# Query weights loaded in the last pair of the prompt attention, and the first stream's latents loaded in the query phase

## What is computed

```python
def mla_project(h, pos, p):
    cq, ckv, kr = jnp.split(h @ p['w_in'], [384, 384 + 256], axis=-1)
    cq, ckv = rmsnorm(cq, g_qa), rmsnorm(ckv, g_kva)
    q = (cq @ w_q_up).reshape(B, T, 8, 128 + 64)
    qn = rmsnorm(q[..., :128], g_qn)
    qr = rope(rmsnorm(q[..., 128:], g_qr), pos)
    return qn, qr, ckv, rope(rmsnorm(kr, g_kr), pos)

def mla_sample_mixer(h, pos, past_ckv, past_kpe, p):
    qn, qr, ckv_new, kr_new = mla_project(h, pos, p)
    ckv_all = jnp.concatenate([past_ckv, ckv_new], axis=1)
    kn = rmsnorm(einsum('bkl,lhd->bkhd', ckv_all, w_uk), g_kn)
    o = mla_attend(qn, qr, kn, kr_all, ckv_all, pos, k_pos)   # softmax over keys
    return einsum('bqhl,lhd->bqhd', o, w_uv) @ w_o
```

## The time and the profile before

| | |
|---|---|
| profiled execution, its own time | 2899.37 us |
| its span | 2897.5 us |
| TensorE busy | 2742.1 us, 95% of the span |
| VectorE, ScalarE, GpSimd busy | 1842.4, 1143.5, 890.8 us |
| granted TensorE clock, mean | 0.983 |

### The profile page before, as it was taken

How to read it: one execution, slowest core, us unless ns; L and a number is a source line. 1 busy time by engine, 2 the same in 40 slices (tenths; PEclk the granted TensorE clock), 3 DMA queues, 4 the chain that set the end, 5 groups by cost and what they waited for, 6 DMA issues and landing times.

```text
span 2897.5 us, 46606 instructions
## 1 busy us (share of the span) xinstructions
PE 2742.1 (95%) x15902; PEld 2455.4 (85%) x15902; DVE 1842.4 (64%) x3070; ACT 1143.5 (39%) x2373; POOL 890.8 (31%) x970
## 2 busy tenths in 40 slices
PE   7889998779998999999999999999999999999998
PEld 4878777678887799999998988888889998989997
DVE  4577787545555567676767677323576767676685
ACT  3355555424444234343434323323233434344331
POOL 1122011036664003433434254000002435253435
PEclk9999999879999999999999999999999999999999
DMA  5144334322223421111111139114521111111118
GB/s 216 55 174 163 120 130 140 107 71 66 65 82 118 152 88 44 43 43 43 43 43 43 43 78 267 64 44 138 175 95 44 43 43 43 43 57 44 43 58 145
DMA packets 121468, 255.10 MB, mean 88 GB/s; under 512 B 16036, under 2 KB 66116, under 8 KB 118024
## 3 DMA queue, kind: packets, MB, share of 16 engines
q1 hardware_dynamic: 112408, 221.70, 22.9%
q0 software_dynamic: 8944, 31.86, 5.0%
HBM read 213.39 MB, written 40.12 MB: 87 GB/s over the span
## 4 chain that ended last, share of the span: by engine, by line
PE 64%; DVE 1%; DMA 1%; SPq 1%; issue 0%; POOL 0%; ACT 0%; POOLq 0%; DVEq 0%; ACTq 0%
PE psum L109 21%; PE psum L111 21%; PE psum L110 21%; PE psum L3033 1%; PE psum L3174 1%; PE psum L3185 0%; PE psum L3148 0%; DMA scratch_x_mid<-half_x 0%; DMA gate_wu_raw<-in_cm_w_in 0%; SPq L2189 0%; DMA half_m<-scratch_mixT 0%; DVE half_out L2786 0%; DVE half_w_lo L2655 0%; DMA half_x<-in_x 0%; SPq L2184 0%
## 5 line engine op out<-in xcount | busy, mean ns | idle before, releaser
L109 PE MATMUL psum<-half_hT_hi,half_w_hi 128*128 128x384 f32 x1536 | 513.7, 334 | 0.0
L111 PE MATMUL psum<-half_hT_hi,half_w_lo 128*128 128x384 f32 x1536 | 513.4, 334 | 0.0
L110 PE MATMUL psum<-half_hT_lo,half_w_hi 128*128 128x384 f32 x1536 | 513.3, 334 | 0.0
L2537 POOL TENSOR_TENSOR half_acc<-half_acc,half_upd 128x512 f32<-128x512 f32 x312 | 422.8, 1373 | 33.5 <-ACT half_upd L2306 28.9
L111 PE MATMUL psum<-half_w_hi,half_s_lo 128*128 128x512 f32 x1040 | 405.7, 390 | 0.0
L110 PE MATMUL psum<-half_w_lo,half_s_hi 128*128 128x512 f32 x1040 | 405.6, 390 | 0.0
L109 PE MATMUL psum<-half_w_hi,half_s_hi 128*128 128x512 f32 x1040 | 405.3, 390 | 0.0
L2753 DVE TENSOR_TENSOR half_acc<-half_acc,psum 128x512 f32<-128x512 f32 x416 | 279.4, 682 | 80.9 <-PE psum L111 80.8
L2289 ACT ACTIVATE half_s_raw<-psum 128x384 f32<-128x384 f32 (+2 forms) x256 | 97.7, 407 | 563.8 <-PE psum L111 563.8
L109 PEld LDWEIGHTS psum<-half_hT_hi,half_w_hi 128*128 128x128 f32 x1536 | 288.3, 188 | 1.2
L110 PEld LDWEIGHTS psum<-half_hT_lo,half_w_hi 128*128 128x128 f32 x1536 | 288.3, 188 | 1.2
(11 more groups left out here) (406 smaller groups left out, 5776.0 us busy)
## 6 DMA issues: line engine op xcount, KB each, us to landing
half_w_raw<-in_w SPq DMA_DIRECT2D x64, 512.0 KB, 4.2
half_w_raw<-in_w SPq DMA_DIRECT2D x128, 256.0 KB, 3.5
patt_mod_w<-in_ada_w_ffn SPq DMA_DIRECT2D x32, 768.0 KB
patt_mod_w<-in_ada_w_att SPq DMA_DIRECT2D x16, 1024.0 KB, 5.6
half_m<-scratch_mixT SPq DMA_DIRECT2D x18, 512.0 KB, 5.0
satt_lT_raw<-in_cacheT SPq DMA_DIRECT2D x32, 256.0 KB, 3.0
satt_l_raw<-in_cache POOLq DMA_DIRECT2D x32, 256.0 KB, 3.5
half_w_raw<-in_w_o SPq DMA_DIRECT2D x16, 512.0 KB, 5.5
```

The source lines that it names most:

```text
L109: pe.matmul(out, a_hi, b_hi, start=first, stop=False)
L110: pe.matmul(out, a_hi, b_lo, start=False, stop=False)
L111: return pe.matmul(out, a_lo, b_hi, start=False, stop=last)
L2537: pool.tensor_tensor(part, part, a.upd[n % UPDS][:], ALU.add).then_inc(a.added, 1)
```

## The change

- A new object `Ahead` holds four tiles and their 14 semaphores, made before the prompt attention, and does their loads. `Phase.ended` leaves those semaphores out of what is cleared.
- In the prompt attention's last pair, after the store of group 3, SyncE loads the query weights (4 chunks) and the key weights (2 pieces), 3.3 MB.
- In every pair, SyncE's store of adaLN step 3, with the load of the next pair's first table, stands after the store of group 6 instead of after that of group 7.
- The query phase starts with the query chunks instead of the key weights. Its per-head work is cut into two halves of four heads: root, normalisation, rotation, transposes, eviction, and product with `wukT`. The sums of squares stand between the splits. The keys' sum, root and `rn_wide` come after the queries'. SyncE loads the constants first, then `wukT`, then stream 0's latents and rope keys (8 loads), which the sample attention no longer loads.
- In the sample attention, VectorE's `split_m(0)` moves from the last stream's tile 7 to tile 6. Token tile 3's rows are loaded there, after `m_ready` 2 and before the store of the sample rows, and the first phase of `mlp_stages` no longer loads them for layer 0.
- Tiles have other places in SBUF.

```diff
@@ prompt_attention_phase, SyncE
+                        if g == 3 and last:
+                            sp.wait_ge(proj_ready, 1 + PAIRS * T)
+                            sp.wait_ge(ss_ready, 1 + PAIRS * T)
+                            ahead.load_query_weights(sp, io)
                         if g == 5 and not last:
                             load_mod1_w(p, 4)
-                    store_mod1(p, 3, not last)
+                        if g == 6:
+                            store_mod1(p, 3, not last)
@@ class Ahead
+    def load_query_weights(self, sp, io):
+        for c in range(4):
+            cols = slice(c * 2 * (DN + DR), (c + 1) * 2 * (DN + DR))
+            sp.dma_start(self.wq_raw[:, :, cols], io["w_q"][:, :, cols]).then_inc(self.wq_in[c], 16)
+        for i in range(2):
+            sp.dma_start(self.wuk_raw[:, i, :], io["w_uk"][:, i, :]).then_inc(self.wuk_in[i], 16)
@@ sample_query_phase, SyncE
-                for i in range(2):
-                    sp.dma_start(wuk_raw[:, i, :], io["w_uk"][:, i, :]).then_inc(wuk_in[i], 16)
-                for c in range(4):
-                    sp.dma_start(wq_raw[:, :, chunk(c)], io["w_q"][:, :, chunk(c)]).then_inc(wq_in[c], 16)
-                sp.dma_start(wukT[:], io["w_ukT"]).then_inc(wukT_in, 16)
                 (five constants)
+                sp.dma_start(wukT[:], io["w_ukT"]).then_inc(wukT_in, 16)
+                for q in range(4):
+                    ahead.load_latents(sp, io, 0, q)
+                    ahead.load_positions(sp, io, 0, q)
@@ GpSimd
-                pool.wait_ge(kss_ready, 1)
-                rms(slice(2, 3), kr_ready)
-                pool.wait_ge(ss_ready, 4)
-                rms(slice(0, 2), r_ready)
+                for half in range(2):
+                    pool.wait_ge(ss_ready, 2 * half + 2)
+                    rms(slice(0, 2), heads(half), r_ready)
+                pool.wait_ge(kss_ready, 1)
+                rms(slice(2, 3), slice(0, H), kr_ready)
@@ ScalarE (wq_split, squares and the key weights' loop as before, each in a function)
+                for c in range(3):
+                    wq_split(c)
+                squares(0)
+                wq_split(3)
+                squares(1)
+                (wuk split, i = 0, 1)
+                squares(2)
+                squares(3)
                 (squares of the keys)
-                act.wait_ge(qT_raw, 1)
-                act.activation(qnT[:], ...)
-                act.activation(qrT[0:DR, :, :]..., ...).then_inc(qT_ready, 1)
+                for half in range(2):
+                    act.wait_ge(qT_raw, half + 1)
+                    act.activation(qnT[:, heads(half), :], ...)
+                    act.activation(qrT[0:DR, :, :]...[:, :, heads(half), :], ...).then_inc(qT_ready, 1)
@@ VectorE
+                for c in range(3):
+                    wq_split(c)
+                sums(0)
+                wq_split(3)
+                sums(1)
+                (wuk low parts, i = 0, 1)
+                sums(2)
+                sums(3)
                 dve.wait_ge(const_in, 16 * 5)
-                step.then(dve.tensor_tensor(gg[:], g_qn[:], g_kn[:], ALU.mult))
+                step.run(dve.tensor_tensor(gg[:], g_qn[:], g_kn[:], ALU.mult))
+                tokens_of(0)
+                tokens_of(1)
                 dve.wait_ge(ksq_ready, 1)
                 (sum of the keys' squares, then ckv_f and kr_f)
@@ TensorE
+                (queries, chunks 0 to 3, then the keys)
+                for half in range(2):
+                    pe.wait_ge(qtok_ready, half + 1)
+                    (transposes of four heads, qn and qr)
+                    mm.then_inc(qT_raw, 1)
+                pe.wait_ge(ksq_ready, 1)
                 pe.wait_ge(wukT_in, 16)
+                for half in range(2):
+                    pe.wait_ge(qT_ready, half + 1)
+                    (product with wukT, four heads, two k)
@@ sample_attention_phase, SyncE
-                sp.wait_ge(a.m_ready, 1)
-                load_m(2)
+                for t in (2, 3):
+                    sp.wait_ge(a.m_ready, t - 1)
+                    load_m(t)
@@ VectorE
+                        if t == T - 2 and not nxt:
+                            split_m(0)
                         if t == T - 1 and not nxt:
-                            split_m(0)
                             split_wo(0)
@@ mlp_stages, SyncE
-                    if t + 3 < TT:
+                    if t + 3 < TT and not (a.layer == 0 and t == 0):
                         load_m(a, t + 3)
```

213 lines of the change are left out of this document (113 added, 100 removed).

## The result

| | before | after |
|---|---|---|
| median of the runs | 2901.98 us (2898.24 to 2908.42, 4 runs) | 2867.14 us (2866.97 to 2870.05, 4 runs) |
| profiled execution, its span | 2899.37, 2897.5 us | 2866.97, 2865.3 us |
| TensorE busy; granted clock in the query phase | 2742.1; 0.66 | 2733.6; 0.76 |

The ratio is 0.988, 95% interval 0.9861 to 0.9899. With all later runs the medians are 2903.1 (63 runs of before, its repeats included) and 2869.9 (12 runs of after): 33.2 us.

The account below looks back on a forecast made before the run. TensorE, busy for 95% of the span, was taken as the bound, so only its gaps could be won. 7.0 + 14.4 + 0 + 0.9 + 4.2 = 26.5 us off 2903.1 gave 2877 us, range 2868 to 2888.

Parts of the forecast that it names:

- Part 1: Prompt attention pairs: adaLN store behind group 6 removes TensorE's waits for the table; 7.0 us, bounds 0 and 7.8.
- Part 3: Query phase: earlier start, weights already there and work in halves shorten the chain; 14.4 us booked, bounds 9 and 17.
- collision: Query phase: GpSimd's roots beside VectorE's two-input operations delay the chain; 1 us taken off the gain.
- rival (c): Query phase: TensorE stays warm, narrow matmuls at full clock save 5 us, total 2872; chance 0.08.
- Part 2: Last pair: 3.3 MB of weight loads delay group 4's store, but nobody waits; cost 0, cover 4 us.
- part 4: Sample attention's start: loading stream 0's latents ahead gains nothing, transfers were there already; 0, bounds 0 and +1.
- Part 5: Sample attention's end: `split_m(0)` one tile earlier takes VectorE's 1.22 us off the last tile; 0.9 us, bounds 0 and 1.5.
- part 6: MLP stages' start: token tile 3 loaded earlier removes TensorE's 2.54 us wait and cold start; 4.2 us, bounds 2.5 and 4.5.

Follow-up runs that it names:

- part 6 alone: Only token tile 3's rows loaded earlier, in the sample attention, against the kernel before: 2899.12 us, ratio 0.9987.

## Why the prediction was right and where it was wrong

**Part 1: the term that was mis-sized.** The mechanism is the one described: the wait for the table went, nothing took its place, and the phase started earlier (1.05 us by the trace, 1.4 said). The size, 7.0 with an upper bound of 7.8, was wrong as a bound. I took the waits (6.5) and one cold start (1.3) from the one profiled execution, and that was the cheapest of four: it had half clock behind one wait, two others had it behind all three. I also did not see the second stretch at half clock in the middle of a pair, which goes and comes as well. Against this one profile the cold start gave nothing: it has two stretches in its steps, and after has two. That 7.0 lies near the 6.5 of these two profiles is luck: it counts a cold start that they do not give back. By the runs the part is worth 9.9 us on the mean (6.5 to 13.5), 2.9 above the forecast: the waits, 6.5 to 7.3, and some 1.5 us for each stretch at half clock beyond two.

**From the trace to the median.** The forecast took the sum from one execution's time and added the 3.7 us by which the median lay above it, as if that distance would stay. It did not: it was made largely of these stretches at half clock (median 2903, profiles with 162.6 us in the steps at 2899.4 and with 169.7 at 2907.2), and the change removed those beyond two. This is the same error as part 1's, seen from the median, and not a second one. That the profiled run lay at the low end of before's runs was in sight and should have widened the range downwards.

**Part 3** was right in its path. From the phase's first DMA, forecast and measured: first product 2.8 and 2.6, half 0 ready 16.8 and 17.0, half 1 20.2 and 20.3, eviction of the product 26.8 and 26.4; the gain, 15.4 with part 1's earlier start in it and booked as 14.4 for a collision, was 14.4 + 1.1 = 15.5. So the allowance of 1 us was not needed. The one term that I had as unchanged, the scores behind it, gave 1.2 to 1.8 more: the first of the narrow matmuls ran at full clock (0.62 us for four in after, 0.88 in the earlier trace rows), part of rival (c). The collision was there, but it was GpSimd that stood: its two small steps took 1.04 and 1.06 us beside VectorE's `wuk_lo`, against 0.31 and 0.20 for the keys' later, while the `wuk_lo` took 1.23 as before. The price was an idle time of 0.64 us of VectorE, not 1. By the rule of the Trainium skill ("SBUF — State Buffer", section "Who interferes with whom") VectorE could have stood for two roots, with a gain of 12.1 instead of 14.4; here the trace does not agree. The root of half 1 ran from 559.33 to 560.97, and inside it VectorE's multiplication of two SBUF tiles took 0.69 us, as it did for half 1 at 563.28 with GpSimd idle. At the sample attention's start, above, it was VectorE that stood.

```profile
554.90 1.04 POOL L1212 TENSOR_TENSOR sq_ms<-sq_ss,sq_inv_n 128x8 f32<-128x8 f32 x1 [7.07 <-DVE sq_ss L1273]
...
556.02 1.06 POOL L1213 TENSOR_TENSOR sq_ms<-sq_ms,sq_eps 128x8 f32<-128x8 f32 x1
...
558.91 0.69 DVE L1287 TENSOR_TENSOR sq_qn<-psum,sq_rs 128x512 f32<-128x512 f32 x1 [0.64 <-POOL sq_rs L1214]
...
559.33 1.64 POOL L1214 TENSOR_TENSOR sq_rs<-sq_ms,sq_power 128x8 f32<-128x8 f32 x1
...
559.96 0.69 DVE L1290 TENSOR_TENSOR sq_qn<-sq_qn,sq_gg 128x512 f32<-128x512 f32 x1
...
566.84 0.31 POOL L1212 TENSOR_TENSOR sq_ms<-sq_ss,sq_inv_n 128x8 f32<-128x8 f32 x1 [5.87 <-DVE sq_ss L1313]
```

**Parts 2, 4, 5, 6** were right in size: 0, 0, 0.9 (said 0.9) and 4.2 (said 4.2), each by an experiment of its own, parts 4 and 5 by a single profile each. Part 2's cover was 2.8 us and not 4. In part 4 "the transfers were there" was true by a hair: ScalarE's high part had waited 2.05 us for them, and started at 612.42, 0.5 us before the low part. Part 5's reason was only half right: GpSimd's short step in the last tile is still 1.27 us in after; what went is the lengthening of the root behind it.

The parts by their means, 9.9 + 1.1 + 14.3 + 1.6 + 0.9 + 4.1, make 31.9 us against the 26.5 of the forecast: 2.9 more in part 1, 1.0 in part 3 and 1.6 in the scores behind it, 0.1 less in part 6. The pooled medians differ by 33.2. The last 1.3 us are within what L0 and L3 do by chance.

## What to carry to other kernels

A wait of TensorE has two prices: its own length, which hardly changes, and the clock behind it and later in the same pair, which one profile may show at full and the next at half. Take two or three profiles of the kernel before costing waits of 2 us and more, count the stretches at half clock in each and in the kernel after as well, and put their price (some 1.5 us each here) in the upper bound; a profiled execution at the low end of the runs may be the cheap case. And before moving an instruction because it is long, see which engine's instruction ends together with it.

## What the runs showed of the hardware

- Behind idle times of 1.7 to 2.8 us TensorE came back at 2.4 GHz in some executions and at 1.2 GHz in others, at the same place of the same program (product 1.53 or up to 2.79 us). The longest wait with full clock behind it was 2.68 us (part 6 alone), the shortest with half clock 2.06 (third profile of before).
- A second stretch at 1.2 GHz came some 41 us later in the pair, with a wait before it or without (clock 0.50 in both rows above); each stretch cost a step some 1.5 us.
- A 128 KB store issued behind 3.3 MB of loads on SyncE's queue landed 8.4 us after its issue (9.4 in after) instead of 1.7. The Trainium skill ("DMA: Bandwidth & Descriptors", section "Queues, rings and completion order") says that a DMA engine takes the descriptors of one issuing engine's ring in order, and that the signal of a landing comes only after that DMA engine's earlier writes; this trace agrees, with 7.9 us.
- GpSimd and VectorE stood for one another in both directions: VectorE's cast of 0.29 us took 1.95 beside a GpSimd memset of 1.81, though the memset reads nothing; GpSimd's step of 0.2 to 0.3 us took 1.04 beside VectorE's two-input subtraction, which itself kept its 1.23. GpSimd's root of 1.64 us and VectorE's two-input multiplication of 0.69 inside it did not lengthen one another.
